# Earlier page turns, exponentials inside slot 15, and tanh gates in a hybrid decoder step on one core

## The reference, cut to what matters

```python
z = rms_norm(x, attn_norm) @ w_in                  # 2048 -> 5120 columns
q, k = rms_norm(z[q part], q_norm), rms_norm(z[k part], k_norm)
v = z[v part]
a, g = jnp.split(z[last 2048 columns], 2, axis=-1)
h = a * jax.nn.sigmoid(g)                          # the gates
c = depthwise_conv(concat([prev, h]), dw_w) + dw_b # 31 taps
c = silu(layer_norm(c, conv_ln_g, conv_ln_b))
p = softmax(q @ k^T / 8)                           # 16 half-heads, prompt: causal
o = (p[even half-heads] - lam * p[odd half-heads]) @ v
x = x + concat([rms_norm(o) * 0.8, c]) @ w_out
x = x + relu(rms_norm(x) @ w_up) ** 2 @ w_down
```

## Time and profile before

| | us |
|---|---|
| median of three runs | 1725.25 |
| the three runs | 1725.25, 1730.4, 1723.85 |
| the profiled execution | 1730.82 |
| its span, first to last instruction | 1729.2 |
| PE busy in the span | 1542.3 (89%) |
| DVE busy | 1018.6 (59%) |
| ACT busy | 617.7 (36%) |
| POOL busy | 420.3 (24%) |

### The profile page before, as it was taken

How to read it: one execution, slowest core, us unless ns; L and a number is a source line. 1 busy time by engine, 2 the same in 40 slices (tenths; PEclk the granted TensorE clock), 3 DMA queues, 4 the chain that set the end, 5 groups by cost and what they waited for, 6 DMA issues and landing times.

```text
span 1729.2 us, 32531 instructions
## 1 busy us (share of the span) xinstructions
PE 1542.3 (89%) x11299; PEld 1365.7 (79%) x11299; DVE 1018.6 (59%) x1504; ACT 617.7 (36%) x955; POOL 420.3 (24%) x654
## 2 busy tenths in 40 slices
PE   6988788777787776669999999999999999999998
PEld 4987565454554543428999999999999999999998
DVE  3477666998999487934355544454444454455444
ACT  4333232122121454433344443343433443334332
POOL 4880477566556554400000000000000000000000
PEclk9998898999989787879999999999999999999999
DMA  6744599999899675755445554555545554555553
GB/s 177 238 132 117 147 315 346 300 306 322 290 308 306 194 227 177 220 191 168 147 152 156 167 167 162 170 162 166 167 162 169 162 166 166 162 169 162 166 166 131
DMA packets 163840, 340.45 MB, mean 197 GB/s; under 512 B 33915, under 2 KB 33971, under 8 KB 163168
## 3 DMA queue, kind: packets, MB, share of 16 engines
q1 hardware_dynamic: 120592, 267.29, 48.2%
q0 software_dynamic: 43168, 72.15, 13.9%
HBM read 334.00 MB, written 5.96 MB: 197 GB/s over the span
## 4 chain that ended last, share of the span: by engine, by line
PE 70%; DVE 18%; issue 5%; ACT 3%; DMA 2%; POOL 1%; POOLq 1%; DVEq 0%; SPq 0%; ACTq 0%
PE acc L569 20%; PE acc L571 20%; PE acc L570 20%; DVE k_page L1434 4%; DVE conv L1403 4%; PE aux L638 3%; DVE w_lo L1293 2%; DMA v_page<-in_cache_v 1%; ACT w_hi L959 1%; DVE tmp L1526 1%; PE acc L587 1%; DVE z L1607 1%; PE aux L686 1%; ACT prob L1102 1%; ACT s_rows L1048 1%
## 5 line engine op out<-in xcount | busy, mean ns | idle before, releaser
L1293 DVE TENSOR_TENSOR w_lo<-raw,w_hi 128x1024 fp32r<-128x1024 f32 x368 | 451.1, 1226 | 524.2 <-ACT w_hi L959 523.0
L959 ACT CAST w_hi<-raw 128x1024 fp32r<-128x1024 f32 x368 | 386.0, 1049 | 705.4 <-PE acc L571 705.3
L569 PE MATMUL acc<-a_hi,w_hi 128*128 128x288 f32 (+1 forms) x1920 | 591.8, 308 | 12.2 <-DVE z L1300 6.8
L570 PE MATMUL acc<-a_lo,w_hi 128*128 128x288 f32 (+1 forms) x1920 | 578.2, 301 | 0.0
L571 PE MATMUL acc<-a_hi,w_lo 128*128 128x288 f32 (+1 forms) x1920 | 577.9, 301 | 0.0
L569 PEld LDWEIGHTS acc<-a_hi,w_hi 128*128 128x128 f32 x1920 | 368.6, 192 | 61.7 <-issue 53.0
L483 POOL DMA_DIRECT2D k_page<-in_cache_k x512 | 332.7, 650 | 291.8 <-PE aux L638 174.0
L570 PEld LDWEIGHTS acc<-a_lo,w_hi 128*128 128x128 f32 x1920 | 369.0, 192 | 0.5
L571 PEld LDWEIGHTS acc<-a_hi,w_lo 128*128 128x128 f32 x1920 | 368.6, 192 | 0.0
L571 PE MATMUL acc<-h_hi,w_lo 128*128 128x288 f32 x1024 | 302.2, 295 | 0.0
L570 PE MATMUL acc<-h_lo,w_hi 128*128 128x288 f32 x1024 | 301.5, 294 | 0.0
(11 more groups left out here) (216 smaller groups left out, 998.4 us busy)
## 6 DMA issues: line engine op xcount, KB each, us to landing
k_page<-in_cache_k POOLq DMA_DIRECT2D x512, 128.0 KB, 5.2
v_page<-in_cache_v SPq DMA_DIRECT2D x128, 512.0 KB, 6.7
raw<-in_w_up SPq DMA_DIRECT2D x128, 512.0 KB, 3.7
raw<-in_w_down SPq DMA_DIRECT2D x128, 512.0 KB, 3.6
raw<-in_w_in SPq DMA_DIRECT2D x80, 512.0 KB, 5.4
raw<-in_w_out SPq DMA_DIRECT2D x32, 512.0 KB, 3.6
x_nat<-in_x_prompt SPq DMA_DIRECT2D x3, 1024.0 KB, 9.4
out<-y_nat SPq DMA_DIRECT2D x8, 256.0 KB, 2.7
```

The lines of the kernel that those rows point to most:

```text
L569: mm(out, wh, ah, start=(kt == 0), stop=False)
L570: mm(out, wh, al, start=False, stop=False)
L959: nc.scalar.copy(w_hi[:, j % SPL], raw[:, j % RAW]).then_inc(hi_ok, 1)
L1293: v.tensor_tensor(w_lo[:, j % SPL], raw[:, j % RAW], w_hi[:, j % SPL].bitcast(F32), ALU.subtract)\
```

## The change

It has six parts.

1. **First pages earlier.** Pages 0 to 7 of sequence 0 are turned beside visits 1 to 3 (three a visit, DVE), the queries are selected in visit 3, and the first two groups of scores are made in slots 7 and 12 of visit 3. The scalar `lam` is worked out in visits 0 and 1 and not ahead of visit 4.
2. **Turns four slots ahead.** In slot j of every body DVE turns page j + 4, in slots 12 to 15 the first four pages of the next sequence. The scores of group g come at the start of slots 0, 4, 8 and 12, the maximum two slots later. Visit 4 has a list of its own: turns of pages 8 to 15 and of four pages of sequence 1, scores of groups 2 and 3 at slots 5 and 10.
3. **Exponentials in slot 15.** The common maximum is made in slot 15, and ACT makes the exponentials at the end of slot 15, ahead of the last piece of the slot work and of the rounding of the next visit's second chunk.
4. **Tanh gates.** sigmoid(g) = (tanh(g/2) + 1)/2: the factor 1/2 goes into the taking of visits 4 and 6 (`take_half`), so a gate is one tanh on ACT and one instruction on DVE. For the silu the layer norm's gain and shift are halved beforehand, and the same one instruction replaces three. The taps begin two slots earlier in visits 6 and 8, and come four a slot in visits 7 and 9.
5. **Turn to rows.** ACT copies the left half of each row block and DVE the right half.
6. **POOL.** The samples' new taps and the causal mask are made after the fourth page of sequence 5 is issued. The mask moves to `c_prod`. The rest of the pages and the stores follow.

```diff
+EARLY = 3
+LEAD = 4
+SCORES = {SG * g: g for g in range(NG)}
+FIRST_TURNS = {0: 8, 1: 9, 2: 10, 3: 11, 5: 12, 6: 13, 7: 14, 8: 15, 11: 16, 12: 17, 13: 18, 15: 19}
+TURNS = {j: j + LEAD for j in range(N_PAGES)}
...
@@ gpsimd
-            with pool.Fori(1, PAIR_V + 1) as s:
+            with pool.Fori(1, PAIR_V) as s:
                 for j in range(N_PAGES):
                     load_keys(s, j)
+            for j in range(SG):
+                load_keys(PAIR_V, j)
+            pool.wait_ge(gate_v, 8)
... (the four new taps and the mask, as before, but here)
+            for j in range(SG, N_PAGES):
+                load_keys(PAIR_V, j)
             for j in range(KS):
                 load_keys(PAIR_V + 1, j)
...
@@ tensor
+            for kt in range(KT):
+                products(EARLY, kt, a_hi, a_lo, 0, T)
+                if kt == 3:
+                    norm_sums(EARLY)
+                if kt == 7:
+                    pe.wait_ge(nrm_root, MT * (EARLY - 1) + 1)
+                    score(0, 0)
+                if kt == 12:
+                    score(0, 1)
...
                 for j in range(N_PAGES):
-                    if ks is not None and j and j % SG == 0:
-                        score(ks, j // SG - 1)
+                    if ks is not None and j in scores:
+                        score(ks, scores[j])
...
-                if ks is not None:
-                    score(ks, NG - 1)
...
-                            pe.wait_ge(nat_a, b - 3)
+                            pe.wait_ge(nat_d if half else nat_a, b // 2 - 1)
...
@@ scalar
-                if beside:
-                    beside(N_PAGES)
-                if n is not None:
-                    hi(n + 1, 1)
                 if ks is not None:
-                    group(NG - 1)
                     act.wait_ge(nm_ok, ks + 1)
                     for g in range(NG + 1):
...
                         fn(keys, keys, ACT.Exp, bias=neg_max[:, 0:1], accum_out=s_sum[:, g:g + 1]).then_inc(exp_ok, 1)
+                if beside:
+                    beside(N_PAGES)
+                if n is not None:
+                    hi(n + 1, 1)
...
-                        fn(tmp[:, m, :], tmp[:, m, :], ACT.Exp, scale=-1.0).then_inc(gate_e, 1)
+                        fn(tmp[:, m, :], tmp[:, m, :], ACT.Tanh, scale=0.5).then_inc(gate_e, 1)
...
@@ vector
+            def turn(p):
+                dve.wait_ge(k_in[p % KS], 64 * (p // KS + 1))
+                keys = k_page[:, p % KS].rearrange("p g q c -> p (g q c)")
+                v.transpose(keys, keys).then_inc(kt_ok, 1)
...
+            for n in range(1, EARLY + 1):
+                def early(i):
+                    if 3 * (n - 1) + i < KS:
+                        turn(3 * (n - 1) + i)
+                    if n == EARLY and i == 1:
+                        select_queries()
+                norm_visit(n, early)
...
+                    if ks is not None and j in turns and N_PAGES * ks + turns[j] < N_PAGES * N_SEQ:
+                        turn(N_PAGES * ks + turns[j])
...
-                    if ks is not None and j % SG == 0 and j:
-                        group(j // SG - 1)
+                    if ks is not None and j in maxes:
+                        group(maxes[j])
...
                 dve.wait_ge(gate_e, m + 1)
-                v.tensor_scalar(g, g, 1.0, None, ALU.add).then_inc(gate_v, 1)
-                dve.wait_ge(gate_v, 3 * m + 1)
-                v.reciprocal(g, g).then_inc(gate_v, 1)
-                dve.wait_ge(gate_v, 3 * m + 2)
-                v.tensor_tensor(t, t, g, ALU.mult).then_inc(gate_v, 1)
+                v.scalar_tensor_tensor(t, g, 1.0, t, ALU.add, ALU.mult).then_inc(gate_v, 1)
```

More of the change, by code:

```diff
@@ L746, in last_norms @@
                     new_scores()
-            body(0, None, ATT_FIRST, end=last_norms, new_at=13)
+            body(0, None, ATT_FIRST, end=last_norms, new_at=13, scores=FIRST_SCORES)
             for s in range(PAIR_V):
@@ L984, in _ @@
             sqrt(root[0:48, 2:3], sums[0:48, 2:3], D).then_inc(sq_x, 1)
-            for j in range(2, NC):
+            for j in range(2, 5):
+                hi(0, j)
+            act.wait_ge(lam_v, 2)
+            fn(lam_exp[:], lam_sum[:], ACT.Exp).then_inc(lam_a, 1)
+            for j in range(5, NC):
                 hi(0, j)
@@ L988, in _, with norm_visit @@
             hi(1, 1)
-            with act.Fori(1, ATT_FIRST) as n:
+            def norm_visit(n, between=None):
                 for m in range(MT):
@@ L1408, in go_on, with body @@
                     next(work, None)
-            def body(ks, vs, n, beside=None, finish=None, first=False):
+            def body(ks, vs, n, beside=None, finish=None, first=False, turns=TURNS, maxes=MAXES):
                 def group(g):
@@ L1548, in _ @@
                 body(s + 1, s, n, beside_visit(n), lambda: take_visit(n))
+            b = 1
+            for base, row, parts in ((16, 0, NAT), (8, 0, NAT), (24, 32, ((T_P - 32, 32), (T_P, N_SMP)))):
+                for i, (_, n) in enumerate(parts):
+                    buf, slot = (v_nat, (i + 1) % 4) if base == 16 else (k_nat, i if base == 8 else i + 2)
+                    dve.wait_ge(nat_mm, b + 1)
+                    v.tensor_copy(buf[row:row + n, slot, 512:1024], acc[0:n, b % 4, :]).then_inc(nat_d, 1)
+                    b += 2
+                    go_on(work, 1)
             go_on(work, CONV_S * TAPS)
-            dve.wait_ge(gate_v, 24)
+            dve.wait_ge(gate_v, 8)
             v.memset(q_st, 0.0).then_inc(zq_ok, 1)
```

219 lines of the change are left out of this document (119 added, 100 removed).

## The result

| | before | changed |
|---|---|---|
| median | 1725.29 (5 runs, 1723.85 to 1730.69) | 1711.76 (5 runs, 1710.0 to 1714.15) |
| ratio, 95% interval | | 0.9914 [0.9893, 0.9935] |
| profiled execution | 1730.82 | 1713.65 |
| its span | 1729.2 | 1711.9 |
| DVE busy in the span | 1018.6 | 986.9 |

The change is faster, by 13.5 us; the range forecast (1632 to 1686) doesn't hold it. The profiled executions differ by 17.2 us. DVE lost 31.7 us of work and the span 17.3, so 14.4 us of it came back as idle time of DVE.

The account below looks back on a forecast made before the run. PE bounds the last 940 us, unchanged; ahead of it DVE bounds visits 6 to 9, DMA visit 5, waits visit 4. Terms sum to -67.5 us: 1663 profiled, 1658 median; own range 1645 to 1670, with rivals 1632 to 1686.

Parts of the forecast that it names:

- Visits 6 to 9: Visits paced by DVE: shorter gates and fewer waits for scores, less longer starts, save 16 us (bounds 0 to -32).
- 5.5 of them inside the visits, which go since the maximum comes two slots later: In visits 6 to 9, 5.5 us of DVE's 13.0 us of waits for the copied scores vanish.
- The boundaries: Visit starts: three grow 4 us each as DVE awaits scores behind `q_cur`; visit 7's stays about 14; visit 9's end gains 4.5.
- Visit 5: Already at the DMA's rate, so it gains only 2 us (0 to -4).
- The floor of the DMA: A visit beside attention moves 21.0 MB, which at 346 GB/s and a share of 1.05 takes 60.6 us.
- The third rival: Exponentials in slot 15 delay ACT's next rounding; only visits 4 and 5 wait, 2 us each; no chance given.
- Visit 4: Earlier scores and pages shorten its chain of waits from 61.3 to 38 us, -23 us (-13 to -28).
- the walk by slots: Visit 4: slots 0 to 5 about 11 us, a 4 us wait in slot 8, slots 8 to 15 16 us.
- The prompt's attention: Shorter silu and four fewer turns: first body -3 us, second -13 (-8 to -18), with 3 repaid for early scores.
- The start of a visit costs nothing: Rival, chance 0.18: PE is ahead of DVE, so visits 6 to 9 lose 32 us, giving 1642.
- The DMA or the front holds back: Rival, chance 0.30 together: late pages give about 1672, visit 4 saving only 13 gives 1668, both 1682.
- the change doesn't do what it says: Rival, chance 0.03: queues keep the old pace, visit 4 and the ends pay back the gates, 1720 to 1730.

Follow-up runs that it names:

- e7: The kernel before with the tanh gates alone, everything else at its place: 1707.6 us, ratio 0.9883.
- e2: The changed kernel with ACT's rounding of a chunk ahead of the copy of the scores in slots 4, 8 and 12: 1698.5 us, ratio 0.9842.
- e15: The kernel before with ACT's rounding ahead of the copy of scores and the first three maxima two slots later: 1716.3 us, ratio 0.9921.
- e1: The changed kernel with `q_cur` and `s_cur` for the next sequence copied in slot 15, not at the next body's start: 1690.2 us, ratio 0.9789.
- e6: The changed kernel with the edits of e1 and e2, and the next sequence's first scores ahead of the closing row on PE: 1662.8 us, ratio 0.9613.
- e4: The changed kernel loading only half the columns of each values page (first four pages whole), so its output is wrong: 1706.5 us, ratio 0.9879.
- e11: e6 with DVE's four reciprocals of visit 4 made one a slot: 1660.9 us, ratio 0.9588.
- e9: The changed kernel without parts 2 and 3 in its regular bodies (no turns four slots ahead): 1676.6 us, ratio 0.9699.
- e13: e9 with ACT's rounding ahead of the copy of scores and the first three maxima two slots later: 1664.3 us, ratio 0.9627.

## Why the prediction was wrong

**Visits 6 to 9 (-16 forecast, +2.1 measured).** The term had three pieces. The gates were right: DVE has 18.6 us less work (18.5 forecast), and e7 turns 16.2 of them into time. The other two pieces counted 2.7 us more of idle time on DVE; measured are 20.7.

- *"5.5 of them inside the visits, which go since the maximum comes two slots later".* This step failed by 13 us. Inside the visits DVE had waited 5.5 us for `s_rows` and 2.6 for `w_hi`, 8.1 in all; after, it waits 15.6 for `w_hi`. I asked who waits for the copy of the scores, and didn't ask what is queued behind it on ACT. The rounding stood there before, too, hidden behind DVE's wait for the same copy; a later maximum took that wait away, and with it, as I read the order, the 0.6 us of work with which DVE had filled the time of the rounding. e2 shows the link (15.6 to 0.6 us, 13 us of time), e15 that it was on the path before the change.
- *The boundaries (+4, +4, +0.7, +4, and -4.5).* Mechanism, place and length were right: a wait of PE for `q_cur`, 9.3 us from there to DVE's copy (9.5 forecast, though its terms add up to 9.7), 13.6 us from the last tap of visit 7 to that copy (about 14), waits of up to 6.8 us at `pT`. The size of the sum was not: I took 4 us for a boundary, and measured are 24.5 us in four waits against 2.6 before, less the 7.5 of the ends of visits 7 and 9, that is +14.4 and not +8.2. e1 and e6 show that what is bought there is real time.

**Visit 5 (-2 forecast, +7.8 measured).** The floor of the DMA was right (e1 has 61.7 us at 350 GB/s and a share of 1.05, had 346). What failed is that the term had nothing for a late start, and a stage that is full all through doesn't make one good. At the end of visit 4 ACT waits for the common maximum (its table load of 1.28 us is over 1.2 us before and costs nothing), then the exponentials hold it; the rounding behind them comes at 214.49, and `q_cur` stands on DVE behind the `w_lo` that waits for it. This is the changed kernel there:

```profile
208.87 1.28 ACT L1083 ACT_TABLE_LOAD   x1 [0.83 <-DVE s_rows L1508]
...
211.24 1.61 DVE L1572 SCALAR_TENSOR_TENSOR z<-acc,rstd 128x304 f32<-128x304 f32 x4
211.35 0.72 ACT L1083 ACTIVATE s_rows<-s_rows,neg_max 128x512 f32<-128x512 f32 x1 [1.20 <-DVE neg_max L1520]
...
214.49 1.03 ACT L989 CAST w_hi<-raw 128x1024 fp32r<-128x1024 f32 x1
215.55 1.23 DVE L1330 TENSOR_TENSOR w_lo<-raw,w_hi 128x1024 fp32r<-128x1024 f32 x1 [2.71 <-ACT w_hi L989]
...
217.23 0.78 DVE L1407 COPY q_cur<-q_sel 32x32 f32<-32x32 f32 x4
...
218.11 3.64 PE L659 MATMUL aux<-k_page,q_cur 128*32 128x512 f32 x16 [6.91 <-issue]
```

The third rival had this wait of 2.7 us (2 forecast) in the right place, and put it "within the range". It didn't see that PE's whole queue and POOL's page requests follow `q_cur`.

**Visit 4 (-23 forecast, -15.2 measured).** POOL asks for the second pages at 150.5 us (148 forecast). Of the 8 us missed, 2.5 are the wait behind the reciprocals, 6.5 us where I had 4; 3.9 are the second half of the walk by slots, which gave it 16 us. It took 19.9, as slot 8 ran at the lower clock and the samples' scores and a wait of 0.7 us had no place in it. The last 1.4 us were not taken apart:

```profile
178.38 7.78 DVE L1551 RECIPROCAL tmp<-tmp 128x304 f32<-128x304 f32 x4
...
190.06 1.18 DVE L1330 TENSOR_TENSOR w_lo<-raw,w_hi 128x1024 fp32r<-128x1024 f32 x1
...
191.30 0.62 PE L586 MATMUL acc<-a_hi,w_hi 128*128 128x304 f32 x1 [6.51 <-DVE w_lo L1330]
```

e11 gives 3.4 us of it back, so the cause is shown for that part and argued for the rest.

**Turn to rows (-5.5, -6.4) and last values (-3, -4.2)** were right, and there is no wait for the mask left.

**The prompt's attention (-3 and -13 forecast, +2.8 and -7.0 measured).** DVE's work in the second body fell by 19.6 us (66.09 to 46.53, 45 forecast). The body kept 75.8 us. The scores stand ahead of all else here, too, and DVE's largest waits are the second copies to `pT`, then the copies of the prompt's output (5.1 us):

```profile
DVE pT L1494 <- PE aux L683: 10.8, 2, 7.3
```

I had counted 3 us for that, in this body alone. Without the lead all from the end of the visits to the output projection is 6.3 us shorter (e9). Which of the chain's links holds the rest in these two bodies was not taken apart.

**The rivals.** "The start of a visit costs nothing" was wrong by its own row. "The DMA or the front holds back" had 1672 to 1682 for two of the things that did happen (visit 4 and full engines), but e4 shows that visits 6 to 9 were held by the chain and not by bytes. None of them had the case that came: that a part which removes no work (the lead) costs more than the part which does brings. The nearest was "the change doesn't do what it says" (1720 to 1730). Without parts 2 and 3 the kernel takes 1676.6 (e9), inside the range; so the step that put the time outside is the price of the lead: 35 us, where the prediction had 2.7 us more of waits in visits 6 to 9 and 3 in the prompt's attention. Even e9 is 19 us above the forecast of 1658; 6 of them are visit 4, the rest was not taken apart. The low end of the range doesn't add up: its terms give 1635 and not 1632, which changes nothing here.

## What to carry to other kernels

Where a wait is to go because its reader comes later, look at what is queued behind the waited-for instruction on its own engine: the next reader of that queue inherits the wait. An instruction moved to the head of a stage makes its latest input the start of everything behind it, on the engines whose requests it frees as well, and where the DMA engines were full all through the stage, the late start was not made good (visit 5: 69.1 us, and 61.7 with `q_cur` in time). So move the input (here four small copies, 1 us of DVE, worth 21 us) before you move the consumer.

## What the runs showed of the hardware that I had not expected

PE pays twice for standing still. The same 16 score matmuls take 1.92 us where PE was busy ahead of them and 3.64 us after a wait of 3 to 7 us, at a granted clock of 0.50, the 1.2 GHz level. It needn't be the last wait that lowers the clock. Ahead of visit 8 it was low before the wait for `q_cur` began, after 4 us in which PE was busy for 0.62, waiting for pages of values:

```profile
414.00:418.00 4.00, 0.62 (x8) 0.13 (x8) 3.97 (x11) 1.19 (x3) 2.37 (x5) 1.00 1.05 324
418.00:424.00 6.00, 2.09 (x12) 1.08 (x12) 5.87 (x18) 4.38 (x13) 0.24 (x1) 0.51 0.91 319
424.40:428.00 3.60, 3.60 (x17) 0.68 (x17) 2.35 (x3) 0.00 (x0) 0.00 (x0) 0.50 0.96 358
```

In visits 6 to 9 the mean granted clock is 0.89 in the changed kernel, 0.94 in e9 and 0.96 in e13, in this window:

```profile
278.10:523.70 245.60, 204.67 (x1631) 137.39 (x1629) 238.10 (x454) 61.06 (x105) 171.63 (x266) 0.96 1.03 340
```

PE's busy time is 216.7, 209.3 and 204.7 us for the same products and scores. So some 12 us of PE's time between the changed kernel and e13 go with the clock's level, and come with the waits that are taken out. The relation is loose (the kernel before has 219.9 us at 0.91), and no run changed the clock alone. The DMA engines gave 350 GB/s over a whole visit (e1, visit 5), where the earlier trace rows has 346 over 36 us. The Trainium skill, "DMA: Bandwidth & Descriptors", Specifications, has about 358 GB/s for a core, and this row is 2% under it. And a tanh gate on DVE is 0.46 us (0.53 taken), with no table load on ACT beside it in the changed kernel's gates.
